# Adding the shift to the token rows of the experts: five VectorE additions replaced by TensorE products

## The chip, the cores and the metric

The kernel runs on one core of one Trainium2 chip. The metric is the device time of one execution in microseconds. It is given as the median of three runs, and the trace is that of one further execution, taken by the hardware profiler. TensorE multiplies matrices (the trace has its matmuls as PE and its loads of the stationary operand as PEld), VectorE is DVE, ScalarE is ACT, GpSimd is POOL, and SyncE (SP) issues most of the DMAs.

## What is computed

One layer of a hybrid trunk for 128 context tokens and 512 latent tokens, 640 rows of 1024 channels. After the token mixers and their residual, each token is normalised and modulated, and goes through a mixture of 16 experts of which two are chosen for each token. Cut to the part that the change touches:

```
h = rms_norm(x, norm_g[1]) * (1 + sc2) + sh2     # sc2, sh2: one row for context, one for latent tokens
scores = sigmoid(h @ w_router)
... group-limited top 2 of 16, weights w ...
for e in range(16):
    a = silu(h @ w_exp_gate[e]) * (h @ w_exp_up[e])
    y = y + combine[:, e:e+1] * (a @ w_exp_down[e])
```

The sh2 in the first line is the shift. The last step of the layer adds y to x through a gate, and a final norm follows.

## The kernel before, in words

Everything is float32 in effect. Large products are split in a high and a low part and made as three products of the type fp32r. Small ones are plain f32 products. The program has three long stages. The projections, the attention and the recurrent branch take the first 505 us. The merge and the output projection go on to 784 us. The experts run from 811 us to 1136 us and a short tail follows. The change lies between the last two, in the router, which here means all that stands between the last matmul of the output projection and the first matmul of the first expert.

Activations are held with channels on partitions. `xa` is x1 times norm_g times (1 + sc2), not yet divided by the root mean square of its token, and x1 is the residual stream. The tile of x1 has the name `xres` in the trace. Each expert gathers its tokens as rows from DRAM, so both have to be turned into rows: `hrow` (640 rows of h, which go to the DRAM tensor `h2d`, in the trace `h_rows`) and `x1t` (rows of x1, used in the tail).

The program is written with explicit semaphores and each engine runs its own list in the written order. In the router these lists are:

- TensorE (from L1059): `to_rows(0, xa, ...)` turns xa in ten groups, two for each of the five tiles of 128 tokens. A group is four transposes of 128 by 128 into one PSUM bank. Four banks are used in turn, so group g waits until ScalarE has emptied group g - 4 (`tr_ev`). Then come the rank products (L1064 to L1068), which need VectorE's one-hot rows `ohsH`. Then come groups 10 to 13, which turn the first four groups of x1, the two sets of inverse products (L1074), which need `ohP` and `ohV`, groups 14 to 19, and, once every group has been emptied, the transposes of the first gathered rows (L1084) and the first expert (L1094).
- ScalarE: it empties the ten groups of xa into `hrow` with the scale `rs5`, which is one over the root mean square (L1480). Then it empties groups 10 to 13 into `x1t` (L1482), makes the high part of the first Wu (L1466, `weights_high(1, 0)`), and empties groups 14 to 19.
- VectorE: a chain of some forty short instructions, from the sums of the squares at L1970 to the slot lists at L2095. Among them stand the five calls of `shifted(t)` (L2010 to L2013). Each adds the shift row to one tile of `hrow` and releases that tile's store to DRAM with `slot_ok`. The shift rows are in `shb`, one for context and one for latent tokens, the same on all partitions.
- SyncE (L577 to L587): the loads of the first Wu and Wd, 2 MB each, the five stores of `hrow`, then the load of the second Wg and the ones after it.
- GpSimd: after the last `low` it waits for the slot lists (`idx_ok`) and for all five stores (`hrow_out`), then issues the gathers of the first two experts (L679).

Of the kernel before, what the change touches and what calls it, by code (L numbers as in the profile page):

```python
# [22 lines left out]
ALU = mybir.AluOpType  # L23
# [3 lines left out]
P = 128  # L27
D = 1024
# [4 lines left out]
TT = T // P  # L33
# [81 lines left out]
def build(nc, xT, cT, w_ada, w_ada_late, b_ada, norm_g, final_g, wtiles, par_in, pack, biasd, w_router, r_bias,  # L115
# [3 lines left out]
    def region(start):  # L119
        at = [start]  # L120

        def put(name, shape, dt=F32):
            t = nc.alloc_sbuf_tensor_at(name, [P] + shape, dt, offset=at[0])
            at[0] += (2 if dt is F16 else 4) * int(np.prod(shape))
            at[0] = (at[0] + 31) // 32 * 32
            assert at[0] <= 229368, (name, at[0])
            return t
        put.at = at
        return put
# [98 lines left out]
    hrow = region(h0 + 4 * KT * T)("hrow", [TT, D])  # L228
# [6 lines left out]
    x1t_at = p3.at[0]  # L235
    x1t = p3("x1t", [TT, D])
    xa = region(p3.at[0])("xa", [KT, T])
# [29 lines left out]
    ms5, rt5, rs5 = p5("ms5", [TT]), p5("rt5", [TT]), p5("rs5", [TT])  # L267
# [15 lines left out]
    sqa = [psq(f"sqa{i}", [T]) for i in range(2)]  # L283
    sqS = psq("sqS", [T])
    shb = region(x1t_at + 4 * (TT - 2) * D)("shb", [2, D])
    po = region(hS_at + 4 * KT * T)
    triH, onesH = po("triH", [P], F16), po("onesH", [P], F16)
    shl = po("shl", [TT, E])
# [17 lines left out]
    PS = ctx.enter_context(nc.psum_tensor("PS", [P, 8, 512], F32))  # L306

    def C(name):
        a, n = CAT[name]
        return cst[:, a:a + n]  # L310
# [7 lines left out]
    ones_ok, x2_in, sx_ok, xs_ok = sem("ones_ok"), sem("x2_in"), sem("sx_ok"), sem("xs_ok")  # L318
# [5 lines left out]
    sq_ok, ss_mm, ms_ok, rt_ok = sem("sq_ok"), sem("ss_mm"), sem("ms_ok"), sem("rt_ok")  # L324
# [16 lines left out]
    xa_ok, sqa_ok, sqs_ok, lg_mm = sem("xa_ok"), sem("sqa_ok"), sem("sqs_ok"), sem("lg_mm")  # L341
    Wg0_in, sh_mm, sh_ok, h2_pre = sem("Wg0_in"), sem("sh_mm"), sem("sh_ok"), sem("h2_pre")
    tr_mm, tr_ev, slot_ok = sem("tr_mm"), sem("tr_ev"), sem("slot_ok")
# [111 lines left out]
    def _(sp):  # L455
# [124 lines left out]
        for g in range(2):  # L580
            sp.dma_start(g2d[g * KT:(g + 1) * KT, :], g2T[g:2 * KT:2, :]).then_inc(gb_in, 16)
        for t in range(TT):
            sp.wait_ge(slot_ok, t + 1)
            sp.dma_start(h2d[t * P:(t + 1) * P, :], hrow[:, t, :]).then_inc(hrow_out, 16)
        load(0, 1, 1)
        for x in (1, 2):
# [43 lines left out]
    @block.gpsimd  # L630
    def _(pool):
        nc.gpsimd.memset(ones[:], 1.0).then_inc(ones_ok, 1)
        for hh in range(2):
            for ty in range(3):
                x = nc.gpsimd.memset(tab[:, hh, ty, 256:384], 0.0)
        x.then_inc(ones_ok, 1)
        nc.gpsimd.memset(csilp[:], 0.0).then_inc(ones_ok, 1)

        def low(n, b):

            pool.wait_ge(w_hi, n + 1)
            wait(pool, half_mm, 2 * (n - 1))
            nc.gpsimd.tensor_tensor(wLo[b][:], wRaw[b][:], wHi[b][:].bitcast(F32), ALU.subtract).then_inc(w_lo, 1)  # L643

        def high0(n):

            pool.wait_ge(raw_in[n], 16)
            nc.gpsimd.tensor_copy(wHi[n][:], wRaw[n][:]).then_inc(w_hi, 1)

        high0(0)  # L650
        low(0, 0)
        pool.wait_ge(ada0_mm, ADA0 // 2)
        nc.gpsimd.memset(xpad[:], 0.0)
        nc.gpsimd.memset(gx[:], 0.0).then_inc(pool_done, 1)
        high0(1)
        low(1, 1)
        low(2, 0)
        with nc.gpsimd.Fori(1, (N1 + N2 + N3 - 2) // 2) as j:
            for b in range(2):
                low(2 * j + b + 1, 1 - b)  # L660
        low(N1 + N2 + N3 - 1, 1)
        nc.gpsimd.memset(onesH[:], 1.0).then_inc(ones_ok, 1)
        nc.gpsimd.tensor_copy(triH[:], C("tri")).then_inc(ones_ok, 1)

        pool.wait_ge(idx_ok, 1)
        pool.wait_ge(hrow_out, 16 * TT)
        seq = Seq(pool, pool_seq)

        def gather(t, b):
            wait(pool, ht_mm, t - 1)  # L670
            seq.step(nc.gpsimd.tensor_copy(idxc[b][:], idxI[:, bass.ds(t, 1)]))  # L671
            seq.last()
            pool.sem_inc(ticks, 1)
            nc.gpsimd.indirect_dma_start(out=hS[b][:], out_offset=None, in_=h2d,
                                         in_offset=bass.IndirectOffsetOnAxis(ap=idxc[b][:], axis=0)) \
                .then_inc(hs_in[b], 16)

        for b in range(2):
            nc.gpsimd.indirect_dma_start(out=hS[b][:], out_offset=None, in_=h2d,  # L679
                                         in_offset=bass.IndirectOffsetOnAxis(ap=idxI[:, b:b + 1], axis=0)) \  # L680
                .then_inc(hs_in[b], 16)
        more = spill_pairs(pool)
        gather(2, 0)
        gather(3, 1)
        with nc.gpsimd.Fori(0, more + (E // 2 - 2)) as j:
            seq.enter(j, 2)
            for b in range(2):
                gather(2 * j + 4 + b, b)
        seq.leave(more + (E // 2 - 2))
        seq.step(nc.gpsimd.tensor_copy(group2[:], groupI[:, bass.ds(2 * more + (E - 2), 2)]))  # L690
        pool.wait_ge(slot_ok, TT + 1)
        pool.wait_ge(zero_row, 16 * (SPILL + 3))
        pool.wait_ge(gb_in, 32)
        seq.last()
        for i in range(2):
            pool.wait_ge(ht_mm, 2 * more + (E - 1 + i))
            pool.sem_inc(ticks, 1)
            nc.gpsimd.indirect_dma_start(out=G2s[i][:], out_offset=None, in_=g2d.rearrange("(g k) c -> g (k c)", g=2),
                                         in_offset=bass.IndirectOffsetOnAxis(ap=group2[:, i:i + 1], axis=0)) \
                .then_inc(hs_in[i], 16)  # L700
        def first_rows(t):

            nc.gpsimd.indirect_dma_start(out=G[t][:], out_offset=None, in_=yd,
                                         in_offset=bass.IndirectOffsetOnAxis(ap=slotI[:, 0, t:t + 1], axis=0)) \
                .then_inc(gy_in[t], 16)

        def second_rows(t):

            pool.wait_ge(gy_in[t], 16)
            nc.gpsimd.indirect_dma_start(out=G[t][:], out_offset=None, in_=yd,  # L710
                                         in_offset=bass.IndirectOffsetOnAxis(ap=slotI[:, 1, t:t + 1], axis=0),
                                         compute_op=ALU.add).then_inc(gy_in[t], 16)

        def gated(t):

            pool.wait_ge(gy_in[t], 32)
            nc.gpsimd.tensor_tensor(G[t][:], G[t][:], g2b[1][:], ALU.mult).then_inc(pool_done, 1)

        pool.wait_ge(W_lo_ok[1], 2 * more + E)
        for b in range(2):  # L720
            pool.wait_ge(ys_out[b], 16 * more + 8 * (E - 2))
        pool.sem_inc(ticks, 1)
        for t in range(TT - 1):
            first_rows(t)
        pool.wait_ge(W_lo_ok[2], 2 * more + (E - 1))
        pool.sem_inc(ticks, 1)
        first_rows(TT - 1)
        for t in range(TT):
            second_rows(t)
        pool.wait_ge(gb_in, 64)  # L730
        for t in range(GATED_DVE, TT):
            gated(t)
# [3 lines left out]
    def _(pe):  # L736
        mm = nc.tensor.matmul
# [310 lines left out]
        def to_rows(half, src, groups):  # L1048
            for gi in groups:
                g = 2 * TT * half + gi  # L1050
                if g >= 4:
                    pe.wait_ge(tr_ev, g - 3)
                for t in range(4):
                    k = 4 * (gi % 2) + t
                    x = nc.tensor.transpose(PS[:, row_bank[g % 4], t * P:(t + 1) * P],
                                            src[:, k, gi // 2 * P:(gi // 2 + 1) * P], C("ident"))
                x.then_inc(tr_mm, 1)

        to_rows(0, xa, range(2 * TT))  # L1059

        pe.wait_ge(ones_ok, 5)
        pe.wait_ge(g2T_ok, 1)
# [4 lines left out]
        for d in range(1, TT):  # L1067
            x = mm(PS[:, 5, d * E:TT * E], onesH[:], ohsH[:, 0:(TT - d) * E], start=False, stop=(d == TT - 1))  # L1068
        x.then_inc(rk_mm, 1)
        to_rows(1, x1, range(4))  # L1070
        for n in range(2 * TT):
            if n % TT == 0:
# [494 lines left out]
    def _(dve):  # L1567
        v = nc.vector
# [436 lines left out]
        rank4 = in_rank[:].rearrange("p t (g x) -> p (t g) x", x=4)  # L2005
        st(v.tensor_reduce(rank4, pair_gt[:], AX, ALU.add))
        seq.last()
        dve.wait_ge(h2_pre, 48)

        def shifted(t):  # L2010

            dve.wait_ge(tr_ev, 2 * (t + 1))
            v.tensor_tensor(hrow[:, t, :], hrow[:, t, :], shb[:, min(t, 1)], ALU.add).then_inc(slot_ok, 1)  # L2013

        st(v.scalar_tensor_tensor(top2[:], in_rank[:], 1.5, sel[:], ALU.is_lt, ALU.mult))
        shifted(0)
        shifted(1)
        seq.last()
        gs = gscore[:].rearrange("p t g -> p (t g)")
        st(v.tensor_reduce(gs, top2[:].rearrange("p t (g x) -> p (t g) x", x=4), AX, ALU.add))  # L2020
# [3 lines left out]
            return a.unsqueeze(2).broadcast_to([P, TT, n])  # L2024

        st(v.tensor_reduce(r5[0][:], gscore[:], AX, ALU.max))
        shifted(2)
        shifted(3)
        seq.last()
        st(v.tensor_tensor(gtmp[:], gscore[:], b3(r5[0][:], SP_G), ALU.is_equal))  # L2030
        seq.last()
# [10 lines left out]
            st(v.scalar_tensor_tensor(oh[:, x].rearrange("p t (g x) -> p (t g) x", x=4), rank4, float(x), in4,  # L2042
                                      ALU.is_equal, ALU.mult))
        seq.last()
        shifted(4)
        both = lin[:]
        st(v.tensor_tensor(both, oh[:], sc[:].unsqueeze(1).broadcast_to([P, 2, TT, E]), ALU.mult))
        seq.last()
# [333 lines left out]
```

## Time and profile before

| what | us |
|---|---|
| median of three runs | 1163.31 (1162.08 to 1164.35) |
| the profiled execution, its own time | 1162.84 |
| its span, from the first to the last instruction | 1161.0 |
| TensorE matmuls busy | 1119.6 (96% of the span) |
| VectorE busy | 900.2 (78%) |
| ScalarE busy | 680.1 (59%) |
| GpSimd busy | 284.3 (24%) |

TensorE is busy almost all the time, so the share alone says that it is the bound. That share is an average over stages. In the router, from 784 to 811 us, TensorE waits for others several times, and its clock is at the lower of its two levels for part of the time. A matmul of plain f32 that is no transpose has two records in this trace, each with its own load of the stationary operand, and a transpose has one. Durations of matmuls include a pipelined end, so the pitch of matmuls in a row is shorter than the duration of one: read the start of the next row, or divide a group's time by its count.

### The profile page before, as it was taken

Reading aid. Unit: us, or ns where it says so; the run is one execution under the profiler, and the core shown is the slowest. Engines: PE = TensorE matmul, PEld = TensorE weight load, DVE = VectorE, ACT = ScalarE, POOL = GpSimd, SP = SyncE. Lnnn points to the kernel's source line nnn. Section 1 sums busy time; section 2 is a strip of 40 time slices with the busy share of each in tenths; the row PEclk is TensorE's granted clock in tenths of the full one; section 3 lists DMA queues with packets and bytes.
Section 4 is the critical chain, followed back from the end, with each engine's and each line's share of the span. In section 5 each row is a group of like instructions: output and inputs, shape, how many; then the busy total and the mean of one; then the engine's idle time right before and its main releaser. Section 6 shows DMA issues by size and latency. Waiting matters only on the chain.

```text
span 1161.0 us, 20317 instructions
## 1 busy us (share of the span) xinstructions
PE 1119.6 (96%) x7300; PEld 1033.1 (89%) x7300; DVE 900.2 (78%) x1267; ACT 680.1 (59%) x1041; POOL 284.3 (24%) x148
## 2 busy tenths in 40 slices
PE   8999999999999999999999999996999999999996
PEld 7899999999999998889999999995788888888874
DVE  4739697978879797867666666638899899999977
ACT  3565757666666757552222222346688787888853
POOL 1232122212212221123333333221111112011035
PEclk9999999999999999999999999997999999999999
DMA  9327422122121212124444436608899999999997
GB/s 374 142 86 223 133 68 74 56 69 86 48 75 59 82 41 82 41 92 146 145 145 145 145 109 236 236 11 339 321 374 424 418 411 411 419 410 413 425 337 188
DMA packets 54876, 233.27 MB, mean 201 GB/s; under 512 B 5368, under 2 KB 22048, under 8 KB 46368
## 3 DMA queue, kind: packets, MB, share of 16 engines
q1 hardware_dynamic: 50352, 216.27, 49.4%
q0 software_dynamic: 4320, 15.73, 4.3%
q8 instruction: 31, 0.51, 0.2%
q10 hardware_dynamic: 144, 0.52, 0.1%
q14 instruction: 29, 0.24, 0.1%
HBM read 211.50 MB, written 21.00 MB: 200 GB/s over the span
## 4 chain that ended last, share of the span: by engine, by line
PE 49%; DVE 4%; DMA 2%; issue 1%; ACT 1%; POOL 0%; SPq 0%; DVEq 0%; ACTq 0%; POOLq 0%
PE PS L1094 25%; PE PS L827 20%; PE PS L1084 1%; DMA adaL<-in_w_ada_late 1%; DVE acc L1833 1%; PE PS L1000 1%; PE PS L1107 1%; DVE hrow L2013 0%; DMA hS<-h_rows,idxI 0%; DVE xo L2263 0%; DVE WgLo L2151 0%; PE PS L941 0%; PE PS L1173 0%; PE PS L932 0%; PE PS L1180 0%
## 5 line engine op out<-in xcount | busy, mean ns | idle before, releaser
L643 POOL TENSOR_TENSOR wLo<-wRaw,wHi 128x1024 fp32r<-128x1024 f32 x80 | 205.5, 2569 | 528.4 <-ACT wHi L1219 528.3
L827 PE MATMUL PS<-hHi,wHi 128*128 128x320 f32 x880 | 279.4, 318 | 1.0 <-issue 0.6
L827 PE MATMUL PS<-hLo,wHi 128*128 128x320 f32 x880 | 272.0, 309 | 0.0
L827 PE MATMUL PS<-hHi,wLo 128*128 128x320 f32 x880 | 271.9, 309 | 0.0
L827 PEld LDWEIGHTS PS<-hHi,wHi 128*128 128x128 f32 x880 | 166.0, 189 | 1.8 <-issue 1.2
L827 PEld LDWEIGHTS PS<-hLo,wHi 128*128 128x128 f32 x880 | 165.7, 188 | 0.0
L827 PEld LDWEIGHTS PS<-hHi,wLo 128*128 128x128 f32 x880 | 165.3, 188 | 0.0
L1833 DVE SCALAR_TENSOR_TENSOR acc<-adaL,csil,acc 128x512 f32<-128x512 f32 x112 | 99.7, 947 | 10.4 <-DMA adaL<-in_w_ada_late 9.8
L1219 ACT ACTIVATE wHi<-wRaw 128x1024 fp32r<-128x1024 f32 x78 | 82.1, 1052 | 28.2 <-PE PS L827 26.0
L2151 DVE TENSOR_TENSOR WgLo<-Wg,WgHi 128x2048 fp32r<-128x2048 f32 x34 | 76.4, 2288 | 12.5 <-ACT WgHi L1466 12.3
L2151 DVE TENSOR_TENSOR WdLo<-Wd,WdHi 128x2048 fp32r<-128x2048 f32 x34 | 76.4, 2287 | 11.3 <-ACT WdHi L1466 11.3
L1688 DVE TENSOR_TENSOR PtLo<-PS,PtHi 128x384 fp32r<-128x384 f32 (+1 forms) x80 | 39.6, 495 | 53.4 <-ACT PtHi L1271 53.4
L2151 DVE TENSOR_TENSOR WuLo<-Wu,WuHi 128x2048 fp32r<-128x2048 f32 x36 | 80.7, 2283 | 0.3 <-ACT WuHi L1466 0.2
L671 POOL COPY idxc<-idxI 128x1 int32 (+1 forms) x16 | 22.5, 1407 | 209.9 <-PE PS L1084 209.9
L1466 ACT ACTIVATE WgHi<-Wg 128x2048 fp32r<-128x2048 f32 x34 | 63.3, 1909 | 16.3 <-DMA Wg<-in_experts 14.4
L1338 ACT ACTIVATE Sb<-Sb,nmax 128x384 f32<-128x384 f32 (+1 forms) x80 | 45.0, 564 | 46.5 <-DVE nmax L1711 46.5
L1699 DVE TENSOR_SCALAR Sb<-Sb,prec 128x384 f32<-128x384 f32 (+1 forms) x80 | 70.6, 924 | 1.4
L1271 ACT ACTIVATE PtHi<-PS 128x384 fp32r<-128x384 f32 (+1 forms) x80 | 35.5, 444 | 58.2 <-PE PS L907 57.7
L1466 ACT ACTIVATE WuHi<-Wu 128x2048 fp32r<-128x2048 f32 x36 | 66.8, 1907 | 1.6 <-PE PS L1094 1.2
L1466 ACT ACTIVATE WdHi<-Wd 128x2048 fp32r<-128x2048 f32 x34 | 63.1, 1907 | 0.0
L1094 PE MATMUL PS<-WgHi,hSH 128*128 128x512 f32 x144 | 56.4, 392 | 2.3 <-DVE WgLo L2151 1.2
L1094 PE MATMUL PS<-WuHi,hSH 128*128 128x512 f32 x144 | 57.8, 402 | 0.0
(380 smaller groups left out, 2855.2 us busy)
## 6 DMA issues: line engine op xcount, KB each, us to landing
wRaw<-in_wtiles SPq DMA_DIRECT2D x80, 512.0 KB, 3.7
Wu<-in_experts SPq DMA_DIRECT2D x18, 2048.0 KB
Wg<-in_experts SPq DMA_DIRECT2D x18, 2048.0 KB
Wd<-in_experts SPq DMA_DIRECT2D x17, 2048.0 KB
adaL<-in_w_ada_late SPq DMA_DIRECT2D x32, 512.0 KB, 4.4
ada<-in_w_ada SPq DMA_DIRECT2D x8, 1024.0 KB, 17.9
slot_rows<-Ys SPq DMA_DIRECT2D x15, 512.0 KB, 10.6
slot_rows<-tab SPq DMA_DIRECT2D x12, 512.0 KB
```

What stands on the lines that cost most here:

```text
L643: nc.gpsimd.tensor_tensor(wLo[b][:], wRaw[b][:], wHi[b][:].bitcast(F32), ALU.subtract).then_inc(w_lo, 1)
L671: seq.step(nc.gpsimd.tensor_copy(idxc[b][:], idxI[:, bass.ds(t, 1)]))
L827: r = mm(PS[:, bank, 0:HALF], w[:, k, :], x[:, k, cols], start=(k == 0 and w is wHi[b] and x is xh), stop=(k == KT - 1 and w is wLo[b]))
L1094: x = mm(out, lhs[l][:, k, :], rhs[r](k)[:, cols], start=(k == 0 and l == r), stop=(k == n - 1 and l == 1))
L1219: A(wHi[b][:], wRaw[b][:], ACT.Copy).then_inc(w_hi, 1)
L1271: A(PtHi[:, 0:nt, hh * P:(hh + 1) * P], PS[:, 6, 0:nt * P].rearrange("p (t q) -> p t q", q=P), ACT.Copy).then_inc(pt_hi, 1)
L1338: A(Sb[(blk + b) % 2][hh][:, 0:w], Sb[(blk + b) % 2][hh][:, 0:w], ACT.Exp, scale=-1.0, bias=nmax[hh][:], accum_out=psumr[:, hh:hh + 1]).th ...
L1466: A(W_hi[x][:, k:k + 4], Wraw[x][:, k:k + 4], ACT.Copy).then_inc(W_hi_ok[x], 1)
L1688: v.tensor_tensor(PtLo[:, 0:nt, cols], PS[:, 6, 0:nt * P].rearrange("p (t q) -> p t q", q=P), PtHi[:, 0:nt, cols].bitcast(F32), ALU.subtra ...
L1699: v.tensor_scalar(x, x, prec[:, hh:hh + 1], None, ALU.mult).then_inc(prob_ok, 1)
L1833: y = v.scalar_tensor_tensor(acc[:, g, :], w, c1, acc[:, g, :], ALU.mult, ALU.add)
L2151: y = v.tensor_tensor(W_lo[x][:, k:k + 4], Wraw[x][:, k:k + 4], W_hi[x][:, k:k + 4].bitcast(F32), ALU.subtract)
```

## The change

Three facts make it equivalent. With r the root mean square of a token, held in `rt5`, and rs5 = 1/r, the old form is hrow = rs5 * xa + shift. The new form is hrow = rs5 * (xa + r * shift). The sum in brackets is made in PSUM by TensorE: the transposes of xa become ordinary f32 products with the identity, and a further product of 512 columns adds diag(r) times the shift rows to the same bank. The scale that ScalarE applies anyway then gives the same rows.

```
     shb = region(x1t_at + 4 * (TT - 2) * D)("shb", [2, D])
+    rtd = region(x1t_at + 4 * 2 * D)("rtd", [TT, P])
...
         for t in range(TT):
-            sp.wait_ge(slot_ok, t + 1)
+            sp.wait_ge(tr_ev, 2 * (t + 1))
             sp.dma_start(h2d[t * P:(t + 1) * P, :], hrow[:, t, :]).then_inc(hrow_out, 16)
...
+        pool.wait_ge(lg_mm, 1)
+        pool.wait_ge(rt_ok, 2)
+        nc.gpsimd.tensor_tensor(rtd[:], C("ident").unsqueeze(1).broadcast_to([P, TT, P]),
+                                rt5[:].unsqueeze(2).broadcast_to([P, TT, P]), ALU.mult).then_inc(ones_ok, 1)
...
-        to_rows(0, xa, range(2 * TT))
+        def xa_rows(gi):
+            if gi >= 4:
+                pe.wait_ge(tr_ev, gi - 3)
+            for t in range(4):
+                mm(PS[:, row_bank[gi % 4], t * P:(t + 1) * P], xa[:, 4 * (gi % 2) + t, tok(gi // 2)], C("ident"),
+                   start=(t == 0), stop=False)
+        def shift_rows(gi):
+            o = gi % 2 * 512
+            mm(PS[:, row_bank[gi % 4], :], rtd[:, gi // 2, :], shb[:, min(gi // 2, 1), o:o + 512],
+               start=False, stop=True).then_inc(tr_mm, 1)
+        for gi in range(4):
+            xa_rows(gi)
+        pe.wait_ge(ones_ok, 6)
+        pe.wait_ge(h2_pre, 48)
+        for gi in range(4):
+            shift_rows(gi)
+        for gi in range(4, 6):
+            xa_rows(gi)
+            shift_rows(gi)
         pe.wait_ge(ones_ok, 5)
         pe.wait_ge(g2T_ok, 1)
         pe.wait_ge(ohs_ok, 1)
...
         x.then_inc(rk_mm, 1)
+        for gi in range(6, 2 * TT):
+            xa_rows(gi)
+            shift_rows(gi)
         to_rows(1, x1, range(4))
...
-        dve.wait_ge(h2_pre, 48)
-        def shifted(t):
-            dve.wait_ge(tr_ev, 2 * (t + 1))
-            v.tensor_tensor(hrow[:, t, :], hrow[:, t, :], shb[:, min(t, 1)], ALU.add).then_inc(slot_ok, 1)
         st(v.scalar_tensor_tensor(top2[:], in_rank[:], 1.5, sel[:], ALU.is_lt, ALU.mult))
-        shifted(0)
-        shifted(1)
...
-        shifted(2)
-        shifted(3)
...
-        shifted(4)
```

The wait of GpSimd for `slot_ok` before the last gathers changes from TT + 1 to 1, because the five increments of `shifted` are gone.

The order of TensorE from the last transposes of xa to the slot lists, before. `cst` is the tile of constants with the identity, and `xres` holds x1:

```order
L1055 MATMUL PS<-cst,xa 128x128 x3
L1064 MATMUL PS<-ohsH,triH 128x80 [waits ohs_ok,g2T_ok,ones_ok]
L1066 MATMUL PS<-ohsH,onesH 128x16 x5
L1068 MATMUL PS<-ohsH,onesH 128x64
L1068 MATMUL PS<-ohsH,onesH 128x48
L1068 MATMUL PS<-ohsH,onesH 128x32
L1068 MATMUL PS<-ohsH,onesH 128x16
L1055 MATMUL PS<-cst,xres 128x128 [waits tr_ev]
L1055 MATMUL PS<-cst,xres 128x128 x3
```

The same place in the changed kernel (`rtd` is the diagonal of the roots, L1069 is in `xa_rows`, L1075 in `shift_rows`):

```order
L1075 MATMUL PS<-shb,rtd 128x512
L1091 MATMUL PS<-ohsH,triH 128x80 [waits ohs_ok,g2T_ok,ones_ok]
L1093 MATMUL PS<-ohsH,onesH 128x16 x5
L1095 MATMUL PS<-ohsH,onesH 128x64
L1095 MATMUL PS<-ohsH,onesH 128x48
L1095 MATMUL PS<-ohsH,onesH 128x32
L1095 MATMUL PS<-ohsH,onesH 128x16
L1069 MATMUL PS<-cst,xa 128x128 [waits tr_ev]
L1069 MATMUL PS<-cst,xa 128x128 x3
L1075 MATMUL PS<-shb,rtd 128x512
```

Before, all ten groups of xa stand ahead of the rank products. Now six stand ahead of them and four between them and the first groups of x1, and each group ends with a product of 512 columns.

The order of VectorE around the first additions, before (`in_rank` and `gscore` are steps of the top-2 choice):

```order
L2015 SCALAR_TENSOR_TENSOR top_198<-in_rank,sel 128x80 [waits h2_pre,dve_seq]
L2013 TENSOR_TENSOR hrow<-hrow,shb 128x1024 [waits tr_ev] x2
L2020 TENSOR_REDUCE gscore<-top_198 128x20 [waits dve_seq]
L2026 TENSOR_REDUCE r_0_202<-gscore 128x5 [waits dve_seq]
L2013 TENSOR_TENSOR hrow<-hrow,shb 128x1024 [waits tr_ev] x2
L2030 TENSOR_TENSOR gtmp<-gscore,r_0_202 128x20 [waits dve_seq]
```

And in the changed kernel:

```order
L2038 SCALAR_TENSOR_TENSOR top_198<-in_rank,sel 128x80 [waits dve_seq]
L2041 TENSOR_REDUCE gscore<-top_198 128x20 [waits dve_seq]
L2047 TENSOR_REDUCE r_0_202<-gscore 128x5 [waits dve_seq]
L2049 TENSOR_TENSOR gtmp<-gscore,r_0_202 128x20 [waits dve_seq]
```

The four long additions are gone from between the short steps, and so is the fifth one further on.

## Rows read from the trace of the kernel before

**Rows 1.** Chain of waits, in order of time: start us, us, what.
```profile
790.83 2.27 DVE hrow L2013 x2
...
793.45 2.27 DVE hrow L2013 x2
...
797.05 1.22 DVE hrow L2013
...
805.42 5.10 DMA hS<-h_rows,idxI
810.65 0.64 PE PS L1084 x4
...
1135.60 1.72 PE PS L1173 x4
```

**Rows 2.** Timeline of TensorE, router: start us, us, line, operands; idle before, releaser.
```profile
784.47 6.42 PE L1055 MATMUL PS<-cst,xa 128*128 128x128 f32 x40
796.86 0.23 PE L1064 MATMUL PS<-ohsH,triH 128*128 128x80 f16 x1 [5.98 <-DVE ohsH L2039]
...
797.21 3.65 PE L1055 MATMUL PS<-cst,xres 128*128 128x128 f32 x16
803.53 0.31 PE L1074 MATMUL PS<-ohV,ohP 128*128 128x26 f16 x5 [2.67 <-DVE ohP L2092]
...
804.75 4.75 PE L1055 MATMUL PS<-cst,xres 128*128 128x128 f32 x24
...
826.47 0.47 PE L1094 MATMUL PS<-WgHi,hSH 128*128 128x512 f32 x1 [1.25 <-DVE WgLo L2151]
```

**Rows 3.** Timeline of VectorE, router, two steps behind the rank products.
```profile
798.78 0.21 DVE L2054 TENSOR_TENSOR over<-PS,cst 128x64 f32<-128x64 f32 x1
...
803.71 0.83 DVE L2092 TENSOR_TENSOR ohP<-cst,where 128x640 f16<-128x640 f32 x1
```

**Rows 4.** Timeline of TensorE, start of the program, ordinary f32 products.
```profile
23.40 2.26 PE L794 MATMUL PS<-cst,rs 128*128 128x128 f32 x10
...
35.50 1.58 PE L765 MATMUL PS<-ones 128*128 128x128 f32 x12
```

**Rows 5.** Stretches: length, each engine's busy us, granted clock, DMA share, GB/s.
```profile
784.70:788.25 3.55, 3.55 (x20) 3.55 (x19) 2.52 (x11) 3.38 (x6) 0.00 (x0) 0.52 1.00 425
788.25:791.00 2.75, 2.64 (x22) 2.17 (x20) 2.65 (x7) 2.75 (x6) 0.00 (x0) 1.00 0.97 417
791.00:795.00 4.00, 0.00 (x0) 0.00 (x0) 3.97 (x6) 1.49 (x3) 0.00 (x0) 1.00 0.96 399
...
796.80:808.70 11.90, 8.42 (x55) 7.95 (x56) 11.02 (x35) 8.04 (x10) 2.98 (x2) 0.50 0.83 298
808.70:812.70 4.00, 1.87 (x16) 1.43 (x14) 2.94 (x3) 2.81 (x6) 1.00 (x2) 1.00 0.79 225
```

**Rows 6.** Timeline of ScalarE, router.
```profile
786.61 5.88 ACT L1480 ACTIVATE hrow<-PS,rs 128x512 f32<-128x512 f32 x10
...
801.39 3.70 ACT L1466 ACTIVATE WuHi<-Wu 128x2048 fp32r<-128x2048 f32 x2
805.88 0.60 ACT L1482 ACTIVATE x1t<-PS 128x512 f32<-128x512 f32 x1 [0.79 <-PE PS L1055]
...
808.44 1.74 ACT L1482 ACTIVATE x1t<-PS 128x512 f32<-128x512 f32 x3 [0.26 <-PE PS L1055]
```

**Rows 7.** Stores of hrow, from issue to landing.
```profile
DMA to landing us min/median/max: 3.1/3.7/3.9
```

**Rows 8.** DMA issues, 812 to 813.5 us: gather of the third expert, us to landing.
```profile
hS<-h_rows,idxc POOLq DMA_INDIRECT x1, 8.5
```

**Rows 9.** Timeline of SyncE's queue, the second Wg.
```profile
798.78 1.07 SPq L573 DMA_DIRECT2D Wg<-in_experts  x1
```

**Rows 10.** The page's costliest groups: mean ns of one GpSimd subtraction.
```profile
L643 POOL TENSOR_TENSOR wLo<-wRaw,wHi 128x1024 fp32r<-128x1024 f32 x80 | 205.5, 2569 | 528.4 <-ACT wHi L1219 528.3
```

More of the change, by code:

```diff
@@ L690, in _ @@
         seq.step(nc.gpsimd.tensor_copy(group2[:], groupI[:, bass.ds(2 * more + (E - 2), 2)]))
-        pool.wait_ge(slot_ok, TT + 1)
+        pool.wait_ge(slot_ok, 1)
         pool.wait_ge(zero_row, 16 * (SPILL + 3))
```

## The prediction, made before the changed kernel ran

> **What bounds the kernel now.** I read the page first: TensorE is at 96% of the span. Then I read the chain of waits in order of time. Outside the router nearly all of it is TensorE's matmuls. In the router it is VectorE, then the gather. The reader is to see there the five additions of the shift, 2.27 + 2.27 + 1.22 = 5.76 us, all on the chain, and behind them the gather of 5.10 us that ends where the first transposes of the first expert start, at 810.65 [rows 1]. The timeline of TensorE shows the other side. It turns xa from 784.47 to 790.9, stands 5.98 us for the one-hot rows, and later stands 2.67 us more [rows 2]. So VectorE bounds this stage and TensorE has room. The stretches add that the room is smaller than it looks. The granted clock is 0.52 (1.2 GHz but for the edge) from 784.7 to 788.25, full after that, and 0.50 again from 796.8 to 808.7, behind four idle microseconds [rows 5]. The change spends TensorE's room to shorten VectorE's list. The question is whether the room is enough.
>
> **What it removes.** Five additions, 5.76 us [rows 1]. Up to the one-hot rows four of them stand, 4.54 us, so `ohsH` would be there by 796.86 - 4.54 = 792.3 [rows 1, 2]. The fifth stands beside the rank products and hides most of its cost no longer. From its first step behind the rank products to its last `ohP` VectorE needs 804.54 - 798.78 = 5.76 us [rows 3].
>
> **What it adds to TensorE.** A transpose costs 6.42/40 = 0.16 us at mixed clock, 3.65/16 = 0.23 at half clock, and 2.64/22 = 0.12 at full clock [rows 2, 5]. An ordinary f32 product of 128 columns has two records. Six of them took 1.58 us at full clock, 0.26 each, and five took 2.26 us mostly at half clock, 0.45 each [rows 4]. A product of 512 columns: two of them, four records, took 1.72 us, 0.86 each [rows 1]. A group was 4 x 0.12 = 0.5 us at full clock and becomes 4 x 0.26 + 0.86 = 1.9 us. Ten groups are 14 us more at the same clock, against 5.98 + 2.67 us of idle time and against transposes that ran slowly.
>
> The timeline comes out thus. The clock in front of 784.7 is not touched, so I keep its fall there, and its rise at 788.25, as behind the same steady work of transposes [rows 5]. Sixteen products of xa: one before the fall, 3.55/0.45 = 8 at half clock, seven at 0.26, done by 790.1. Four shift products, 3.4 us: 793.6. Groups 4 and 5, 3.8 us: 797.4. VectorE's one-hot rows have been there for 5 us, so the rank products start at 797.4, where they started at 796.86. TensorE has used up its idle time at that point and the 4.54 us are gone. Then 0.35 us of rank products, four groups at 1.9: group 9 is done at 805.4. Groups 10 to 13 at 16 x 0.12: 807.3. VectorE has had everything ready since 797.8 + 5.8 = 803.6, but the inverse products stand behind these groups and start at 807.3. Before, both sets were done by 804.75, where the next group follows [rows 2].
>
> **What follows on the other engines.** ScalarE empties a group in 0.59 us (5.88/10) [rows 6] and some 0.7 alone. Group 9 is emptied at 806.2 and groups 10 to 13 at 808.5 (3 in 1.74, 0.58 each). The high part of Wu is next in ScalarE's list, 3.70 us, to 812.2. Only then come groups 14 to 19, 6 x 0.58, to 815.7. TensorE waits for all of them before the first gathered rows. Before, ScalarE ended these at 808.44 + 1.74 = 810.2, just ahead of the gather [rows 6]. On the other way, the last store of `hrow` can go at 806.2, lands 3.1 to 3.9 us later [rows 7], and the gather follows at about 809.9. It lands 5.2 us later at best (805.42 to 810.65, [rows 1]), so at 815.1. The load of the second Wg, which started at 798.78 [rows 9], stands behind that store in SyncE's list and now starts at 806 and runs beside the gather. The one gather that ran beside such a load took 8.5 us [rows 8], which would give 818.4. Both ways end near each other. I take 815.9 for the first gathered rows on TensorE, by ScalarE's way and a gather of 6 us: + 5.2 us.
>
> **The edits that cost nothing.** The product on GpSimd is 640 of 1024 elements at 2569 ns [rows 10], 1.6 us. It can start when the roots are there, which is ahead of 786.61, where ScalarE empties the first group with them [rows 6], so it is done by 788.3. TensorE needs it at 790.1. If that cover were gone it would cost at most 1.6 us. The shift rows are in place, as VectorE did not wait for them at 790.8. The stores' new wait comes with the emptied groups and has no VectorE behind it. The later loads shift, but no more than their users.
>
> **Is it given back?** From the first gathered rows on everything hangs in one line: the next stop, 1.25 us for the second WgLo [rows 2], is set by a chain that starts at the first expert's own products. I see nothing that waits for anything else, so the shift stays to the end.
>
> **The clock.** Between 791 and 795 TensorE was idle, and its clock was at 0.50 afterwards [rows 5]. In the changed kernel groups 14 to 17 go at once, by 808.9, and group 18 must wait for ScalarE at about 812.8. That is again a gap of near four microseconds, in front of the first expert. Before, groups 14 to 19 went without a gap, 4.75 us [rows 2], and the clock was full when the first expert began [rows 5]. So I expect that the first expert starts at half clock. After the fall at 784.7 half clock lasted 3.55 us of steady work, after the one near 795 it lasted until 808.7 with gaps [rows 5]. Half of such a time is lost, 1.8 us for the first. The bounds are 0 (no fall) and 3 (six microseconds at half clock). I take 2.0.
>
> The sum is made against the profiled execution's own time: 1162.84 + 5.2 + 2.0 = 1170.0 us. That execution lies 0.5 us below the median of the runs, which is inside their spread, and I do not add it.
>
> **Two rules of the Trainium skill.** The granted clock rose to 1.00 at 788.25 while TensorE had done nothing but transposes since 784.47 [rows 2, 5]. The Trainium skill, page "TensorE: Matmul & The Clock Gate", section "Part 4: PE-mode transpose", says that transposes do not count as work for the clock gate. By that rule products in their place would win the full clock earlier, and the transposes of x1 would let it go. The row disagrees, so I give the change no such gain.
> The ordinary product took 0.26 us against 0.12 for a transpose, 2.2 times [rows 4, 5]. The same page, section "Terms", says that the transpose mode is four times faster for FP32, and the Trainium skill, page "Perfetto Trace Analysis", section "Transposes", asks for real transposes in place of matmuls. Taken literally a product would be 4 x 0.12 = 0.48 us, an estimate from that page's factor. It lies near the third rival below.
>
> **Rivals.**
> 1. The clock does not fall before the first expert. For it: the transposes of x1 stand on both sides of the gap, as at 797 and 801 in the trace before, where the clock simply stayed what it was [rows 5]. Against it: the four idle microseconds before 795 did it [rows 5]. Time: 1162.84 + 5.2 = 1168.0.
> 2. The gather decides, at 8.5 us beside the load of Wg: 818.4 for the first rows in place of 815.9, and the clock low too: 1172.5. For it is the one gather beside such a load [rows 8]. Against it, most of Wg is in by the time this gather starts.
> 3. The products of xa are dear also at full clock, 0.45 each as in the slower row [rows 4]: 32 of the 40 are made at full clock, 32 x 0.19 = 6 us more: 1176. Against it is the row at full clock.
> 4. VectorE remains the bound, since TensorE's products are cheap: if a product of xa costs no more than a transpose (0.16 us in the mixed stretch) and the one of 512 columns 0.43, half of its two records, TensorE has done six groups by 791.4, the rank products start with the one-hot rows at 792.3, `ohP` is complete at 798.5, group 13 is turned before that, and ScalarE ends x1t and Wu some 4.3 us earlier than before: 1158.5. This decides only if six groups end before 795. Rows 1 and 4 both say otherwise.
> 5. The change does nothing that can be measured: TensorE keeps full clock from the start of the router and all else is at its best. The products then end 1.5 to 2 us earlier and the clock never falls: 1162.84 + 2.8 = 1165.6 is as low as I get, at the edge of no change.
>
> **How the numbers follow.** The forecast has 0.44, rival 1 has 0.28, rival 2 has 0.12, rival 3 has 0.04, rival 4 has 0.05, rival 5 has 0.07. A measurement of this kernel can tell 0.2%, 2.3 us, from no change, so slower means above 1165.6. Slower gets 0.88 with all of the first four, faster 0.05, and the same 0.07. The range takes in rivals 1 and 2 and the bounds of the clock term and stops above rival 5: 1166.4 to 1172.8.
>
> **What would show it.** The trace after should have: no idle time of TensorE before the rank products, which start near 797.4; the ordinary products of xa at 0.26 us each behind 788; the shift products at 0.86; VectorE waiting for the rank products and for the inverse ones, about 5 us and 3 us; group 9 emptied near 806; the high part of Wu near 808.5 to 812.2; the first gathered rows on TensorE near 815.9; a granted clock of 0.50 there. The prediction is wrong in its main step if the rank products start clearly before 796, and in its sign if the first gathered rows come before 810.6.

## The result, and the profile after

The changed kernel takes 1170.13 us, median of six runs (1168.68 to 1171.76). The kernel before took 1162.96 beside it (1162.08 to 1166.48). The ratio is 1.0058, with a 95% interval from 1.0041 to 1.0075: it is slower, by about 7 us. The forecast was 1170.0 us. The trace is of the slowest of the six executions, 1171.76 us with a span of 1169.9.

The chain of waits of the changed kernel in the router, in order of time, answers to [rows 1]:

```profile
784.74 5.31 PE PS L1069 x32
790.05 3.44 PE PS L1075 x8
793.48 0.89 PE PS L1069 x8
...
802.59 0.89 PE PS L1069 x8
803.49 0.88 PE PS L1075 x2
804.38 0.70 ACT hrow L1510
805.10 2.90 DMA h_rows<-hrow
808.04 0.83 issue
808.87 7.14 DMA hS<-h_rows,idxI
816.14 1.10 PE PS L1114 x4
...
818.64 4.70 PE PS L1124 x12
```

VectorE is no longer on it. From the last sums of the squares to the last group of xa the chain is TensorE alone, then the last group's emptying, its store, and a gather of 7.14 us. An ordinary product of xa takes 0.89/4 = 0.22 us at full clock and a shift product 0.86.

The timeline of TensorE in the changed kernel answers to [rows 2]:

```profile
796.82 0.20 PE L1091 MATMUL PS<-ohsH,triH 128*128 128x80 f16 x1
...
804.18 1.91 PE L1060 MATMUL PS<-cst,xres 128*128 128x128 f32 x16
805.93 0.41 PE L1104 MATMUL PS<-ohV,ohP 128*128 128x26 f16 x10
806.19 1.94 PE L1060 MATMUL PS<-cst,xres 128*128 128x128 f32 x16
811.15 1.27 PE L1060 MATMUL PS<-cst,xres 128*128 128x128 f32 x8 [3.02 <-ACT x1t L1512]
816.14 1.94 PE L1114 MATMUL PS<-cst,hS 128*128 128x128 f32 x8 [3.71 <-DMA hS<-h_rows,idxI]
...
834.06 0.47 PE L1124 MATMUL PS<-WgHi,hSH 128*128 128x512 f32 x1 [1.25 <-DVE WgLo L2169]
```

The idle 5.98 us ahead of the rank products are gone, and these start at 796.82 where they had started at 796.86. The new idle times, 3.02 and 3.71 us, stand in front of the first expert. TensorE's stop for WgLo, the low part of the second expert's Wg, is 1.25 us as before, 7.6 us later.

The timeline of VectorE answers to [rows 3]. It waits for what it had delayed before:

```profile
797.27 0.22 DVE L2072 TENSOR_TENSOR over<-PS,cst 128x64 f32<-128x64 f32 x1 [3.08 <-PE PS L1095]
...
802.22 0.83 DVE L2110 TENSOR_TENSOR ohP<-cst,where 128x640 f16<-128x640 f32 x1
806.37 0.18 DVE L2113 CAST idxI<-PS 128x26 int32<-128x26 f32 x1 [3.33 <-PE PS L1104]
```

The stretches answer to [rows 5] (length, busy us of each engine, granted clock, DMA share, GB/s):

```profile
784.80:788.10 3.30, 3.30 (x17) 3.30 (x17) 2.48 (x8) 1.83 (x3) 1.25 (x1) 0.50 0.99 417
788.30:808.00 19.70, 19.70 (x136) 14.66 (x134) 12.25 (x48) 9.80 (x15) 0.00 (x0) 1.00 0.64 252
808.30:811.00 2.70, 0.00 (x0) 0.00 (x0) 2.15 (x1) 2.70 (x4) 1.83 (x2) 1.00 1.00 376
812.10:822.20 10.10, 5.83 (x18) 4.38 (x17) 5.30 (x11) 6.12 (x7) 1.15 (x2) 0.50 0.97 365
822.60:826.60 4.00, 4.00 (x32) 3.31 (x31) 4.00 (x10) 1.03 (x1) 1.27 (x1) 1.00 0.15 52
```

The clock is full from 788.3 to past 811, where it had been at half from 796.8 to 808.7. It is at half from 812.1 to 822.2, where it had been full. ScalarE's timeline answers to [rows 6]:

```profile
804.38 0.69 ACT L1510 ACTIVATE hrow<-PS,rs 128x512 f32<-128x512 f32 x1 [1.06 <-PE PS L1075]
804.97 2.05 ACT L1512 ACTIVATE x1t<-PS 128x512 f32<-128x512 f32 x4
806.88 3.74 ACT L1496 ACTIVATE WuHi<-Wu 128x2048 fp32r<-128x2048 f32 x2
810.48 3.06 ACT L1512 ACTIVATE x1t<-PS 128x512 f32<-128x512 f32 x6
```

It is done with x1 at 813.54, 2.6 us ahead of the gathered rows.

Executions differ in the long stages before the router and in the tail. So the router is best compared by distances, counted from the first VectorE step behind the last sums (`ms`, at 784.65 before and 784.78 after). In us:

| from the last sums to | before | before, second trace | changed | changed, second trace |
|---|---|---|---|---|
| last group of xa emptied | 7.8 | 7.8 | 20.3 | 21.6 |
| gather of the first expert issued | 20.8 | 20.8 | 24.1 | 25.3 |
| x1 all emptied | 25.5 | 25.6 | 28.8 | 30.0 |
| first gathered rows on TensorE | 26.0 | 25.9 | 31.4 | 32.7 |
| first matmul of the first expert | 28.0 | 27.9 | 33.9 | 35.2 |
| stop for the second WgLo over | 41.8 | 41.6 | 49.3 | 51.1 |

From the stop to the gathered rows of the sixteenth expert it is 277.5 us before, 277.2 in its second trace and 277.8 in the changed kernel. From there to the end it is 57.1, 59.8 and 58.0. The router's 7.5 us are all kept. The tail varies by 1 to 4 us: it is 57.1 to 61.3 over the twelve traces of this study.

### The profile page after: what moved, and what is told of

The parts are those of the page before. It is cut to its first block, busy times and chain, and to the rows that moved or that the text cites. A ratio compares the mean times of both kernels' runs of the same rounds, so it can differ in the third digit from the quotient of the medians.

```text
span 1169.9 us, 20433 instructions
## 1 busy us (share of the span) xinstructions
PE 1131.3 (97%) x7360; PEld 1040.1 (89%) x7360; DVE 899.2 (77%) x1262; ACT 680.4 (58%) x1041; POOL 286.4 (24%) x149
## 4 chain that ended last, share of the span: by engine, by line
PE 40%; DMA 7%; DVE 4%; issue 2%; ACT 1%; POOL 1%; SPq 0%; ACTq 0%; DVEq 0%; POOLq 0%
PE PS L832 20%; PE PS L1124 16%; DMA Wg<-in_experts 3%; DVE WgLo L2169 1%; DVE acc L1863 1%; PE PS L1114 1%; DMA Wd<-in_experts 1%; DMA adaL<-in_w_ada_late 1%; PE PS L1069 1%; PE PS L1075 1%; DMA G<-slot_rows,slotI 1%; DMA slot_rows<-Ys 1%; PE PS L1005 1%; ACT WgHi L1496 1%; POOL G L708 1%
## 5 line engine op out<-in xcount | busy, mean ns | idle before, releaser
L1863 DVE SCALAR_TENSOR_TENSOR acc<-adaL,csil,acc 128x512 f32<-128x512 f32 x112 | 103.6, 983 | 6.5 <-DMA adaL<-in_w_ada_late 6.1
L1368 ACT ACTIVATE Sb<-Sb,nmax 128x384 f32<-128x384 f32 (+1 forms) x80 | 45.0, 564 | 46.6 <-DVE nmax L1741 46.5
L676 POOL COPY idxc<-idxI 128x1 int32 (+1 forms) x16 | 18.3, 1144 | 216.6 <-PE PS L1114 216.6
```

The lines of the kernel that those rows point to most:

```text
L1368: A(Sb[(blk + b) % 2][hh][:, 0:w], Sb[(blk + b) % 2][hh][:, 0:w], ACT.Exp, scale=-1.0, bias=nmax[hh][:], accum_out=psumr[:, hh:hh + 1]).th ...
L1863: y = v.scalar_tensor_tensor(acc[:, g, :], w, c1, acc[:, g, :], ALU.mult, ALU.add)
```

## The experiments

The kernels were timed on different chips, so their medians are not compared directly: each kernel has its ratio to runs of the kernel before on the same chip. Distances count from `ms` of the same trace, as in the table above, and each kernel has one trace.

### The load of the second Wg held back

```
+        sp.wait_ge(hs_in[0], 16)
         load(0, 1, 1)
```

> The changed kernel, with the load of the second Wg held back until the first gather has landed. Theory A (the gather is slow because that 2 MB load runs beside it): the gather lands in about 5.2 us as before the change, not 7.1, so the first gathered rows reach TensorE near 814.2 in place of 816.1. The clock has fallen near 812 all the same. Time 1170.1 - 1.9 = 1168.2. Rival B (the gather takes 7 us because it follows its own stores so closely): it stays at 7 us and the time at 1170.1. If the load then comes too late for the second expert, the time rises above 1170.1.

Measured: 1167.81 us, ratio 1.0023 (1.0009 to 1.0037), against 1.0058 and 1.0069 for the changed kernel. In its chain the gather is gone, and what stands there is ScalarE's way:

```profile
801.88 0.69 ACT hrow L1511
802.57 1.95 ACT x1t L1513 x4
804.52 3.59 ACT WuHi L1497 x2
808.11 2.93 ACT x1t L1513 x6
811.09 1.13 PE PS L1115 x4
```

The gather landed in 4.4 us, where it had taken 7.1:

```profile
hS<-h_rows,idxI POOLq DMA_INDIRECT x1, 4.4
```

The first gathered rows come 28.8 us behind the last sums and no longer 31.4: 2.6 us, more than the 1.9 expected. The stop for the second WgLo is over at 46.6 in place of 49.3. Theory A holds and B falls: the same stores, just as close, and a fast gather. So the prediction's way over ScalarE is real, but it is the second bound, and the gather beside the load is the first.

### TensorE's gaps filled

`warm(n, 4)` makes n ordinary products of the tile of ones into a PSUM bank that is free. Into the changed kernel, in front of group 18 and in front of the gathered rows:

```
-        to_rows(1, x1, range(4, 2 * TT))
+        to_rows(1, x1, range(4, 8))
+        warm(11, 4)
+        to_rows(1, x1, range(8, 2 * TT))
         pe.wait_ge(tr_ev, 4 * TT)
+        warm(14, 4)
```

> The changed kernel, with 11 ordinary products of the ones tile in TensorE's first gap (between groups 17 and 18) and 14 in the second (ahead of the first gathered rows), into a PSUM bank that nobody reads any more. Theory A (the first expert is slow by the half clock that follows the gaps): the granted clock stays at 1.00 through 812 to 822, the first twelve matmuls of the first expert take 3.06 us in place of 4.70, the next transposes are faster too, and the time falls by 2 to 2.3 us, to 1168. Rival B (the half clock is hidden behind VectorE's low parts of the second Wg): the first matmuls are faster and the time stays at 1170.1.

Measured: 1172.51 us, ratio 1.0069 (1.0047 to 1.0091): no gain. The trace shows an effect that the time hides. It is of the fastest of the six executions, 1168.11 us, and whether the clock kept full in the others is not known. From its chain of waits:

```profile
811.61 3.39 PE PS L770 x28
815.00 0.45 PE PS L1117 x4
...
816.85 3.01 PE PS L1127 x12
```

And the stretch of its first expert, where the clock stays full:

```profile
815.00:822.00 7.00, 6.02 (x44) 4.94 (x42) 5.76 (x11) 5.50 (x5) 1.51 (x3) 1.00 0.80 310
```

The first twelve matmuls take 3.01 us, not 4.70. From the first matmul to the end of the stop for WgLo it is 13.7 us, against 15.4 in the changed kernel and 13.8 before. So the half clock costs 1.7 us behind the first matmul, and nothing behind it hides that. The fourteen products themselves held the gathered rows up: these come at 32.1 in place of 31.4, though the gather, 6.7 us here, had landed by 30.8. The stop ends at 47.8 in place of 49.3, a gain of 1.5 us that six timed runs do not show.

### Only the first gap filled

The same without `warm(14, 4)`.

> The changed kernel with 11 ordinary products of the ones tile in TensorE's gap between groups 17 and 18 alone. The version with 14 more ahead of the gathered rows kept the full clock but held the gathered rows up by some 2 us. Theory A (the half clock costs the first expert 1.6 us and its neighbours 0.5): the clock stays at 1.00, the gathered rows are not delayed, the stop of the second expert ends 2 us earlier than in the changed kernel, time 2 us below it. Rival B (VectorE's chain behind the first expert hides it): the stop ends at the same distance.

Measured: 1171.75 us, ratio 1.0079 (1.0063 to 1.0095), and 1171.91, 1.0069 (1.0050 to 1.0088), for the unaltered changed kernel timed beside it. The gathered rows were not delayed (31.3). The granted clock is 1.00 from 811.0 to 814.8, behind the filled gap, but it fell in the second gap and is 0.50 from 815.0 to 818.0. From the first matmul to the end of the stop it is 15.2 us. My expectation was wrong: filling one of two gaps did not keep the clock, and so this kernel says nothing on what the clock costs.

### Wg held back and the first gap filled

The edit of the first experiment and `warm(11, 4)` together.

> The changed kernel with both: Wg held until the first gather has landed, and 11 products in the first gap. Theory A: both terms add, 2 us each, so the resumption of the second expert comes 45 us behind the last sums in place of 49, time 4 us below the changed kernel and 3 us above before. What is left is the price of the products themselves, by ScalarE's emptying of x1 behind them. Rival B: one of them hides the other and the sum is 2 us.

Measured: 1168.92 us, ratio 1.0050 (1.0035 to 1.0064), 3.0 us below the unaltered changed kernel beside it. The gathered rows come at 28.8 and the stop ends at 46.2. The clock fell here too, at 812.8, just behind the first matmul of the first expert at 812.3, and rose again at about 816. So this is in the main the gain of the held load, 2.6 to 3 us. The filling adds 0.4 us at most: the stop ends at 46.2 and not at 46.6 as with the load alone held. The gain is below the 4 us of theory A and above the 2 us of rival B. No run held the load and filled both gaps.

### The changed kernel again

> The changed kernel unaltered, as the base for the other kernels of this call, since executions differ from chip to chip by several us in the tail. From the last sums of the squares to the first gathered rows on TensorE 31 us, to the resumption of the second expert (the stop for its WgLo) 49 us, against 26.0 and 41.8 in the trace before the change. Ratio to before 1.004 to 1.0075.

Its distances are in the table above. The order of events is the same, 1.2 to 1.9 us later, since the clock rose later among the first products: 32 records took 6.55 us against 5.31. That is the part of the changed kernel that varies with the clock. The kernel before, unaltered:

> The kernel before, unaltered, for a second trace of it. It tells which distances of the router repeat and which depend on where the clock falls: the first gathered rows 26 us and the stop of the second expert 41.8 us behind the last sums if they repeat; 1 to 2 us more in the second if the clock is at half there in this execution. The way from the sixteenth expert to the end, 57.1 us in the first trace, differs between executions by 1 to 4 us whatever the kernel.

Measured 1163.07 us, ratio 0.9997 (0.9977 to 1.0017). All its distances repeat within 0.2 us.

### The shift left out: what VectorE's relief is worth

The transposes of before, no shift products, a short VectorE list. The shift is missing from the rows of the experts.

```
-        for gi in range(4):
-            xa_rows(gi)
+        to_rows(0, xa, range(2 * TT))
         pe.wait_ge(ones_ok, 6)
         pe.wait_ge(h2_pre, 48)
-        for gi in range(4):
-            shift_rows(gi)
-        for gi in range(4, 6):
-            xa_rows(gi)
-            shift_rows(gi)
...
-        for gi in range(6, 2 * TT):
-            xa_rows(gi)
-            shift_rows(gi)
```

> The changed kernel without the shift (it is left out altogether) and with the transposes of the kernel before: VectorE's list is short, TensorE's is as before the change. It tells what the relief of VectorE is worth alone. Theory A: the one-hot rows come 4.5 us and the slot lists 5.3 to 5.8 us earlier than in the kernel before, the last store goes at once, the gather starts near 799.6 or when the stores have landed (about 796.5) and the first gathered rows reach TensorE near 805, unless ScalarE's emptying of x1 is the bound (about 806): time 1163.0 - 4.5 = 1158.5. Rival B (the additions were hidden and VectorE did not bound): 1162 to 1163.

Measured: 1166.02 us, ratio 1.0005 (0.9986 to 1.0023). Theory A fails. The time is near rival B's, but not for its reason, since the additions were not hidden. VectorE did its part: one-hot rows at 8.2 in place of 11.8, slot lists at 15.5 in place of 20.3. But the stores, now released at once, land late. From its DMA issues between 790 and 796 us (KB each, median us to landing), beside [rows 7]:

```profile
h_rows<-hrow SPq DMA_DIRECT2D x5, 512.0 KB, 8.0
Wg<-in_experts SPq DMA_DIRECT2D x1, 2048.0 KB, 13.0
```

And from its chain of waits:

```profile
795.11 8.58 DMA h_rows<-hrow
803.73 0.82 issue
804.56 0.73 POOL hS L684
...
807.14 11.37 DMA hS<-h_rows,idxI
```

The gather is issued at 17.9, not at 12 to 15. The gathered rows come at 23.6, only 2.4 us sooner than before. Two things then take these back. The first expert begins at half clock (0.50 from 810 to 815). And the gather of the second expert, the last line above, takes 11.37 us beside the next load of 2 MB (of Wu, issued at 808.1), so TensorE stands 1.08 us for it, where it had not stood before. The stop for WgLo ends at 42.5, against 41.8. So even a free shift gains nothing that can be measured here. The next bound is the DMAs, which at that time move 4 MB of the first Wu and Wd.

### The shift left out and Wg held back

As the last, and `sp.wait_ge(hs_in[0], 16)` and `sp.wait_ge(hs_in[1], 16)` in front of the load.

> The kernel without the shift (left out), with the transposes of before, and the load of the second Wg held until the first two gathers have landed. Without the holding, the relief of VectorE gave nothing: the stores took 8 us to land beside the loads of the first Wu and Wd and that of Wg, and the gather 5.6 to 8.5 us. Theory A (the relief is eaten by the DMAs that it sets free at the wrong moment, and the Wg load is the larger part): the last store lands 3 us earlier, the gather takes 5 us, the first gathered rows come about 20 us behind the last sums and not 24, and the time is 2 to 4 us below before. Rival B (the first Wu and Wd alone fill the DMAs): stores stay at 7 to 8 us and the time within 1 us of before.

Measured: 1168.73 us, ratio 1.0045 (1.0027 to 1.0062), slower than before. The stores took as long as with Wg beside them:

```profile
DMA to landing us min/median/max: 8.4/8.6/8.7
```

So the load of Wg is not what slows the stores, and rival B is right as far as they go: the loads of the first Wu and Wd are left as the cause. The times of this trace fit it: the load of Wd, issued at 784.17, took 14.1 us and landed at 798.3, and the first store landed at 799.2. I have not taken the loads away, so it is not shown. The stores may also hold up each other: the five are issued within 5.6 us here and within 12.9 in the changed kernel, where they took 2.8 us each. The gather took 5.0 us, against 4.4 with the load held in the first experiment. The gathered rows came at 23.6 again, and the stop ended at 42.1, against 42.5 without the holding. The loss comes elsewhere. Held back until both gathers had landed, Wg and the loads behind it came later, and the chain goes over the load of the third Wg:

```profile
828.91 10.79 DMA Wg<-in_experts
```

This explains a small part: from the stop to the sixteenth expert it is 278.7 us, 1.2 more than before. The rest of the 5 us by which the median lies above before lies in front of the router or in the tail (60.4 us in this trace), where executions differ anyway, and its cause stays open.

### The products alone

The kernel before, with its forty transposes of xa made as ordinary products, the additions still on VectorE:

```
-        to_rows(0, xa, range(2 * TT))
+        for gi in range(2 * TT):
+            if gi >= 4:
+                pe.wait_ge(tr_ev, gi - 3)
+            for t in range(4):
+                x = mm(PS[:, row_bank[gi % 4], t * P:(t + 1) * P], xa[:, 4 * (gi % 2) + t, tok(gi // 2)], C("ident"),
+                       start=(t == 0), stop=(t == 3))
+            x.then_inc(tr_mm, 1)
```

> The kernel before, with the forty transposes of xa made as ordinary f32 products and nothing else: the additions stay on VectorE, no product of 512 columns. Theory A (TensorE had 6 us of room, and the dear part is only dear by its sum with the 512-column products): ten groups end near 784.6 + 8 x 0.44 + 32 x 0.22 = 795.2, still ahead of the one-hot rows, the tiles of hrow come up to 4 us later, the additions wait for them in part, and the time rises by 0 to 2 us: 1163 to 1165. Clock: no fall near 795, which makes the groups of x1 faster than before. Rival B (the products alone are the price): it rises by 5 us or more.

Measured: 1165.34 us, ratio 1.0005 (0.9989 to 1.0021). The last group of xa is emptied at 12.3 and not at 7.8, and the gathered rows come at 26.7 and not at 26.0. TensorE had the room for these, as theory A has it. They were not free, though: the granted clock was 0.62 from 813.0 to 817.5, the first twelve matmuls of the first expert took 4.60 us, and the stop for WgLo ends at 44.1, against 41.8. These 2.3 us lie at the edge of what the interval of the time allows.

```profile
812.66 4.60 PE PS L1100 x12
```

### The changed kernel without its products of 512 columns

`shift_rows` does nothing, and the ordinary products release the group. The shift is left out.

> The changed kernel without its ten products of 512 columns (the shift is left out), everything else as in it: ordinary products of xa, its order, short VectorE list, stores released by ScalarE. Theory A (the ten products of 512 columns, 8.6 us of TensorE, are what pushes the last store out): group 9 is emptied 13 to 14 us behind the last sums and not 20.3, the first gathered rows come near 26 and not 31.4, with the DMAs as the next bound, and the time is that of before within 2 us: 1163 to 1165. Rival B (the ordinary products are the price): group 9 at 18 or later, time 1168 or more.

Measured: 1165.18 us, ratio 1.0008 (0.9994 to 1.0022). The last group of xa:

```profile
796.10 0.69 ACT L1508 ACTIVATE hrow<-PS,rs 128x512 f32<-128x512 f32 x1 [0.21 <-PE PS L1069]
```

That group is emptied 13.4 us behind its last sums (`ms` at 783.43), against 20.3 with the ten products. The gathered rows come at 24.1, 2 us sooner than expected, against 31.4. The stop for WgLo ends at 42.4, against 49.3. So the ten products of 512 columns, 8.6 us of TensorE, are 7.2 us of the way to the gathered rows, and they alone separate this kernel from the changed one.

## Why the prediction was right, and where it was not

**TensorE's room.** Right, as predicted. The idle time was used up: rank products at 796.82 (predicted 797.4), and VectorE stood 3.08 and 3.33 us (predicted about 5 and 3). The first wait is shorter in part because the one-hot rows came 0.9 us later than predicted. Of this, 0.72 us are one addition that stood beside the product on GpSimd, an edit that the prediction had at no cost. The experiments show the parts: without the shift products the room is enough to the gathered rows, with them it is not.

**The price of a product.** Too high. I took 0.26 us from a group of six with its pipelined end, and it is 0.22, 1.9 times a transpose (1.91 us for 16, 0.12 each). The last group of xa was done 1 us earlier than predicted. The shift product was right (0.86).

**What decides behind it.** Here the step failed, though its sum did not. I let ScalarE's way decide and had the gather take 6 us. ScalarE was done at 813.5, not 815.7. The gather was issued at 808.9, not 809.9, and took 7.14 us. The gathered rows came at 816.14, predicted 815.9: the errors cancelled, and that was luck. Holding the Wg load back shows it, since then the gather takes 4.4 us and ScalarE's way decides at 28.8. Rival 2 had this mechanism with a size of 8.5 us.

**The clock.** Right in what it cost. It stayed full through 32 transposes of x1 up to 808.1, fell at 812.1, 1 us after TensorE had resumed behind the first gap, and was full again behind 822.2, and the first twelve matmuls took 4.70 us against 3.01 with full clock. The predicted 2.0 us is 0.5 us ahead of the first matmul (2.5 us from the gathered rows to it, against 2.0) and 1.6 behind it. The two gaps of 3.02 and 3.71 us were predicted as one of four, in front of group 18. The version with only that gap filled lost the clock in the second gap, so the gap that the prediction named is not the only one that matters.

**No giving back.** Right: 7.5 us at the stop, about 7 in the time.

**The sum.** 5.4 + 0.5 + 1.6 = 7.5 us in the trace, 7.2 predicted. That the forecast of 1170.0 lies 0.1 us from the median of 1170.13 is luck too: the six executions spread over 3 us.

**The gain.** The prediction took it that VectorE's 5.76 us were the bound and that only TensorE's price ate them. The version without a shift shows that little of them was to be had even for free: 4.8 us were left at the slot lists, 2.4 at the gathered rows behind the slow stores, and nothing at the next stop (42.5 against 41.8). I had no such step.

## What to carry to other kernels

When a step leaves a bounding engine, look for the room of the one that takes it in us of idle time at that place, not in its share of the span, and price the new instructions by their pitch at the clock granted there. Then ask what the relieved engine releases earlier, and what is on the DMA queues at that moment: here the stores, released sooner, went out behind 4 MB of weights and took twice as long. And where a change turns one long idle time into gaps at another place, look whether the clock is low at the start of the next dense stage.

## What the runs showed that I had not expected

- A VectorE addition was held up while GpSimd made its product `rtd`. The addition, of 80 columns, took 0.96 us and ended within 0.1 us of it. It took 0.96 us in all nine traces with this product and 0.24 us in the three without it. The delay hid here, since VectorE had time. The two lines, of the changed kernel's timelines:

```profile
785.33 1.25 POOL L667 TENSOR_TENSOR rtd<-cst,rt 128x640 f32<-128x640 f32 x1 [16.24 <-ACT rt L1499]
```

```profile
785.72 0.96 DVE L2008 TENSOR_TENSOR sc<-sc,shl 128x80 f32<-128x80 f32 x1
```

- The first gather of 512 KB took 4.4 to 5.0 us with the load of Wg held back (three traces) and 6.7 to 7.3 us beside that load of 2 MB, issued 3.3 us earlier (four traces).
- Filling one of two gaps of TensorE did not keep its clock. Filling both did, in the one trace of it.
- Tails of the same kernel differ by up to 3 us between executions (57.1 and 59.8 us for the kernel before), which hides effects of 1.5 us even in six timed runs. The distances inside a stage repeat within 0.2 us in the kernel before.
